# The mixer's last dense layer (1024 x 1024 x 1024, fp32 in three passes) as four pairs of output tiles of seven half-size products

## What is computed

```python
def _hybrid_mixer(h, w_in, ..., w_diff_out, w_fox_out, w_o, lambda_init):
    ...
    merged = jax.nn.sigmoid(ga) * (ya @ w_diff_out) + jax.nn.sigmoid(gb) * (yb @ w_fox_out)
    return merged @ w_o

def second_block(x, mem, ...):
        x = x + _hybrid_mixer(_rmsnorm(x, g_mix[l]), ...)
        x = x + _memory_cross_attention(_rmsnorm(x, g_mem_q[l]), _rmsnorm(mem, g_mem_kv[l]), ...)
        x = x + _sq_relu_mlp(_rmsnorm(x, g_mlp[l]), w1[l], w2[l])
```

## Time and profile before

| | us |
|---|---|
| median of 3 runs | 2438.28 |
| lowest, highest | 2435.59, 2439.02 |
| span of the profiled execution | 2433.8 |
| TensorE busy in the span | 2394.8 |
| VectorE, ScalarE, GpSimd busy | 1459.3, 951.4, 982.1 |

### The profile page before, as it was taken

One profiled execution on the slowest core, in us unless ns is written; L12 is line 12 of the kernel. 1 busy time (PEld: TensorE's weight loads), 2 busy tenths in 40 slices (PEclk: granted clock), 3 DMA queues, 4 the chain that ended last, 5 costly groups with the idle time before them and its releaser, 6 DMA issues. The chain is left out here.

```text
span 2433.8 us, 33823 instructions
## 1 busy us (share of the span) xinstructions
PE 2394.8 (98%) x12088; PEld 1995.5 (82%) x12088; DVE 1459.3 (60%) x2340; ACT 951.4 (39%) x1759; POOL 982.1 (40%) x776
## 2 busy tenths in 40 slices
PE   9999999999999999999999999999999999999998
PEld 4888888887888888888888888887877888888886
DVE  5865656476464446446454653445576666798878
ACT  4443434344133444434434520234243333444443
POOL 1323132222482222222222232311357666699785
PEclk9999999999999999999999999999999999999999
DMA  8513131223453221222122244211314444644442
GB/s 308 175 35 124 36 106 60 87 72 114 148 191 96 83 60 59 70 84 74 52 74 78 83 139 172 96 52 44 95 48 152 160 160 147 233 161 159 147 148 86
DMA packets 87144, 271.92 MB, mean 112 GB/s; under 512 B 10056, under 2 KB 10184, under 8 KB 82000
## 3 DMA queue, kind: packets, MB, share of 16 engines
q1 hardware_dynamic: 64560, 184.37, 22.7%
q10 hardware_dynamic: 22432, 85.60, 10.9%
HBM read 198.08 MB, written 58.23 MB: 105 GB/s over the span
## 5 line engine op out<-in xcount | busy, mean ns | idle before, releaser
L743 POOL CAST w_hi<-raw 128x1024 fp32r<-128x1024 f32 x112 | 120.5, 1076 | 1079.2 <-issue 369.7
L2999 PE MATMUL ps<-act_hi,w_hi 128*128 128x512 f32 x1248 | 499.0, 400 | 1.9 <-DVE act_lo L2641 1.1
L3001 PE MATMUL ps<-act_hi,w_lo 128*128 128x512 f32 x1248 | 488.5, 391 | 0.0
L3000 PE MATMUL ps<-act_lo,w_hi 128*128 128x512 f32 x1248 | 486.7, 390 | 0.0
L745 POOL TENSOR_TENSOR w_lo<-raw,w_hi 128x1024 fp32r<-128x1024 f32 x112 | 278.0, 2482 | 9.0
L3001 PEld LDWEIGHTS ps<-act_hi,w_lo 128*128 128x128 f32 x1248 | 234.2, 188 | 52.0
L2999 PEld LDWEIGHTS ps<-act_hi,w_hi 128*128 128x128 f32 x1248 | 234.6, 188 | 45.1 <-DVE act_lo L2641 1.5
L3000 PEld LDWEIGHTS ps<-act_lo,w_hi 128*128 128x128 f32 x1248 | 234.9, 188 | 40.6
L3015 PE MATMUL ps<-act_hi,w_hi 128*128 128x512 f32 x384 | 150.2, 391 | 1.6 <-POOL w_lo L745 1.2
L3017 PE MATMUL ps<-act_lo,w_hi 128*128 128x512 f32 x384 | 149.6, 390 | 0.0
L3019 PE MATMUL ps<-act_hi,w_lo 128*128 128x512 f32 x384 | 118.3, 389 | 0.0
(11 more groups left out here) (548 smaller groups left out, 5843.0 us busy)
## 6 DMA issues: line engine op xcount, KB each, us to landing
raw<-in_w_stream_dram SPq DMA_DIRECT2D x192, 512.0 KB, 3.6
x_own_f<-a_dram SPq DMA_DIRECT2D x32, 512.0 KB, 5.7
a_dram<-stage SPq DMA_DIRECT2D x18, 512.0 KB, 6.2
ada<-in_w_ada_dram SPq DMA_DIRECT2D x4, 2048.0 KB, 21.5
spill<-res ACTq DMA_DIRECT2D x16, 512.0 KB, 4.9
gate_dram<-gate_sb ACTq DMA_DIRECT2D x32, 256.0 KB, 2.0
stage<-spill ACTq DMA_DIRECT2D x16, 512.0 KB, 4.1
act_lo_f<-a_dram SPq DMA_DIRECT2D x16, 512.0 KB, 5.4
```

The lines of the kernel that those rows point to most:

```text
L743: nc.gpsimd.tensor_copy(w_hi[:, s, :, :], raw[:, s, :, :]).then_inc(S["w_hi"], 1)
L2999: nc.tensor.matmul(out, wh, xh, start=start, stop=False, skip_group_check=onto)
L3000: nc.tensor.matmul(out, wh, xl, start=False, stop=False, skip_group_check=onto)
L3001: return nc.tensor.matmul(out, wl, xh, start=False, stop=stop, skip_group_check=onto)
```

## The change

The layer `out = W^T X` is cut into 2 x 2 blocks: pairs of output tiles, halves of the channels (k 0 to 3, 4 to 7), halves of the tokens. Each pair takes seven products of 4 k, 128 outputs and 512 tokens in place of eight: with a11, a12 the halves of the first tile's weights and a21, a22 those of the second, s1 = a21 + a22, s2 = s1 - a11, s4 = s2 - a12, s3 = a21 - a11 on the weights, and on the operand t1 = x11' - x12', t2, t3, t5 from the halves of rows j and j+4. The products are numbered; `LP_ORDER = (1, 0, 4, 6, 3, 2, 5)` is the order on TensorE, `PLACE` gives each its bank, and 4, 6 and 5 add onto the banks of 1, 0 and 3.

- **Operand sums** (VectorE, `merged_row`): rows 0 to 3 write one sum each (L2817), rows 4 to 7 three each; of rows 0 to 3 only the left half gets a high and a low part. ScalarE makes highs of the sixteen sums (`t_hi`), GpSimd twelve of the lows (`t_lo`), VectorE four (`t_lows`). The sums lie in `res`, twelve of the highs and lows in memory that the merge's operand occupies until T_MERGE is done.
- **Weight sums** (GpSimd, `block_weights`): four sums and seven lows of 512 columns a pair; ScalarE makes the seven highs (`block_high`), before GpSimd did a cast and a subtraction of 1024 columns a tile. Most lie in the free right halves of `act_hi` and `act_lo` rows 0 to 3. `w_split` rises by two after the last low.
- **Read-out** (VectorE, `block_sums`): six reads of PSUM and three additions a pair; ScalarE copies product 1 out of its bank (`first_copied`) before product 4 adds onto it. x1 rows go to `x1_rows` and `stage` in turn (`x1_load`).
- **ScalarE's order**: the loops of the merge are unrolled and weight highs stand between the sigmoids; in block n it does `first_copied(n)`, squares and spills of block n-1, then all highs of block n+1. The mkv loads move behind the layer. New semaphores share counters of earlier stages (`lw_sum` is printed as qk_ss, `lw_hi` qk_sq, `lt_sum` qk_spread, `lt_hi` qk_perm, `lt_lo` qk_sin, `lp_done` qk_roped, `lp_copied` qk_normed, `lp_ev` df_pt).

```diff
-            split_range(T_MERGE + 2, 8)
-            split_range(T_WO + 2, 8)
+            for t in range(2, 8):
+                split((T_MERGE + t) // 2, t % 2)
+                if 3 <= t < 7:
+                    t_lo(0, t - 3)
+            def block_weights(n):
+                a11, a12, a21, a22 = (quarter(raw, o, h) for o in range(2) for h in range(2))
+                s1, s2, late, s3 = (lw_whole(n, i) for i in (0, 2, 6, 3))
...
+                loaded(0)
+                low(1, a11)
+                if n == 0:
+                    low(4, a12)
+                loaded(1)
+                summed(0, s1, a21, a22, ALU.add)
+                sum_made(0)
+                summed(2, s2, s1, a11, ALU.subtract)
+                if n:
+                    low(0, s1)
+                    low(4, a12)
+                sum_made(2)
+                summed(6, late, s2, a12, ALU.subtract)
...
+                low(3, s3)
+                low(2, s2)
+                if n == 0:
+                    for i, j in T_LOWS[4:]:
+                        t_lo(i, j)
+                pool.sem_inc(S["w_hi"], 2)
+                pool.wait_ge(S["lw_hi"], lw_high_count(n, 5))
+                nc.gpsimd.tensor_tensor(LP_LO[5], a22, LP_HI[5].bitcast(F), ALU.subtract).then_inc(S["w_split"], 2)
...
+                if i == 2:
+                    block_high(0, 1)
+                    block_high(0, 4)
+                    block_high(0, 0)
                 sigmoids(0, 2 * i + 2)
             sigmoids(1, 6)
+            block_high(0, 2)
+            block_high(0, 6)
+            block_high(0, 3)
             merged_hi(0, 6)
+            act.wait_ge(S["spilled"], 128)
+            act.wait_ge(S["tile_done"], T_WO)
+            x1_load(0)
...
+            for i, j in T_HIGHS[4:10]:
+                t_hi(i, j)
+            first_copied(0)
             merged_hi(1, 6)
+            for i, j in T_HIGHS[10:]:
+                t_hi(i, j)
+            block_high(0, 5)
...
+            for n in range(4):
+                if n:
+                    first_copied(n)
+                    for s in range(2):
+                        residual_square("wo", "x2", s, n - 1)
+                        residual_kept("wo", s, n - 1)
+                if n < 3:
+                    for i in (1, 0, 4):
+                        block_high(n + 1, i)
+                    if n:
+                        x1_load(n + 1)
+                    for i in (6, 3, 2, 5):
+                        block_high(n + 1, i)
...
+                read(0, 1, add[:, 1, right], add[:, 1, right], lp_bank(n, 0), ALU.subtract)
+                read(4, 2, res[:, a, left], add[:, 0, left], lp_bank(n, 4), ALU.add)
+                read(6, 3, res[:, a, right], add[:, 0, right], lp_bank(n, 6), ALU.subtract)
+                read(3, 4, add[:, 1, right], add[:, 1, right], lp_bank(n, 3), ALU.add)
+                read(2, 5, part, part, lp_bank(n, 2), ALU.add)
+                nc.vector.tensor_tensor(res[:, a, right], res[:, a, right], part, ALU.add).then_inc(S["lin_evac"], 1)
+                nc.vector.tensor_tensor(add[:, 1, left], add[:, 1, left], part, ALU.add).then_inc(S["lp_part"], 1)
+                nc.vector.tensor_tensor(res[:, b, right], add[:, 1, right], part, ALU.add).then_inc(S["lp_part"], 1)
+                nc.vector.tensor_tensor(res[:, b, left], add[:, 1, left], lp_bank(n, 5), ALU.add
+                                        ).then_inc(S["lin_evac"], 1)
...
-            with pe.Fori(0, 3) as i:
-                linear_pair("wo", T_WO, "merged", i)
-            linear_pair("wo", T_WO, "merged", 3, last=True)
+            def block_product(n, i):
+                out, onto = lp_bank(n, i), i >= 4
...
+                if i == 4:
+                    pe.wait_ge(S["lp_copied"], LEFT["lp_copied"] + n + 1)
+                elif i == 6:
+                    pe.wait_ge(S["lp_ev"], LEFT["lp_ev"] + 5 * n + 1)
+                elif i == 5:
+                    pe.wait_ge(S["lp_ev"], LEFT["lp_ev"] + 5 * n + 4)
+                for k in range(4):
+                    if n == 0 and i in (1, 4):
+                        pe.wait_ge(S["lo_ready"], 8 * FILL["merged"] + k + (1 if i == 1 else 5))
```

## The result

| | before | changed |
|---|---|---|
| median | 2438.26 us | 2453.02 us |
| lowest, highest (4 runs each) | 2435.59, 2439.02 | 2451.61, 2454.36 |
| span of the profiled execution | 2433.8 us | 2451.5 us |
| from the layer's first matmul to the query steps | 111.36 us | 126.46 us |

The ratio is 1.0062, with an interval from 1.0050 to 1.0074: slower, by 14.8 us. The prediction said 2452.1 with a range of 2437.0 to 2459.0.

What follows compares the result with a forecast made beforehand. TensorE, busy for 98% of the 2433.8 us span, was taken as the bound. Terms -10.9 + 7.8 + 6.5 + 3.5 + 5.2 + 1.7 = +13.8 gave a span of 2447.6 and, with 4.5 added, 2452.1 us; range 2437 to 2459.

Steps and rivals of the forecast that it cites:

- Block 0: First block of the layer: TensorE gets 7.8 us of new waiting at products 4 and 6.
- 0.8, 4.6 and 2.4: Block 0's waits in us: product 4 for ScalarE's copy, its k=3 for row 7's low half, product 6 for product 0's read.
- Block 1: Second block: product 4 waits 6.5 us for ScalarE's copy of product 1, which stands behind seven weight highs.
- Blocks 2 and 3: Weights run in a loop of 20.85 us against TensorE's 19.05; each block loses 1.8, together 3.5 us.
- 13.75 + 1.6 + 0.9: Within the weights' loop, in us: eleven GpSimd operations, two hand-overs to ScalarE and back, and meetings with VectorE.
- Into the next layer: From the last block to the query steps: late read, split, row 4 and last square add 5.2 us.
- the 6.0 counted: Waits into the query, in us, before taking off the 0.85 of old waiting that goes, leaving +5.2.
- The clock: Behind the last wait, one fall of the granted clock to half is not absorbed and costs 1.7 us.
- The conversion to a time: Forecast span 2447.6 us plus the kept 4.5 us between span and median of runs gives 2452.1.
- No blocking: Rival: VectorE and GpSimd do not hold each other up; time 2437.4 us, no measurable change; chance 0.15.
- Copy not late: Rival: block 1's weights land by 1480, no product 4 waits, gain nearly whole; 2427 to 2432 us; chance 0.05.
- Longer loop: Rival: GpSimd operations of the weights' loop cost 1.4 us, clock falls are not absorbed; 2457 to 2460 us; chance 0.22.

Runs made afterwards that it cites:

- e4: Changed kernel plus matmuls nobody reads where TensorE waits: 18 in block 0 ahead of row 7's low half, 16 in block 1 ahead of the copy; 2452.5 us, ratio 1.0058.
- e2: Changed kernel with row 6's sigmoid moved ahead of row 5's high, and so ahead of the three weight highs; 2452.0 us, ratio 1.0056.
- e6: Changed kernel with row 6's sigmoid ahead of row 5's high and row 6's high ahead of the weight highs for products 2, 6 and 3; 2454.5 us, ratio 1.0065.
- e1: Changed kernel with GpSimd giving the first raw tile of a block free once s3 is made, not with the last low; 2448.7 us, ratio 1.0051.
- e3: Changed kernel with ScalarE, in blocks 1 to 3, copying product 1 ahead of the highs for products 6, 3, 2 and 5; 2455.7 us, ratio 1.0072.
- e5: Changed kernel plus matmuls nobody reads: 6 ahead of the query's first tile, 5 ahead of the sums of squares; 2453.1 us, ratio 1.0064.
- e7: Changed kernel without GpSimd's eight lows of operand sums 3 and 2; ScalarE writes a copy of each sum instead; 2451.9 us, ratio 1.0058.
- e12: Against an earlier follow-up with reordered lists, VectorE in block 3 makes fewer lows ahead of its read of product 3 and all squares last; 2443.7 us, ratio 1.0028.

## Why the prediction was right

**The sum.** Positions from the layer's start, forecast and measured:

| | forecast | measured |
|---|---|---|
| VectorE starts row 6 | -6.1 | -6.16 |
| row 7's low half ends | 12.1 | 12.5 |
| product 4 of block 1 | 38.7 | 39.19 |
| product 4 of block 2 | 59.6 | 61.08 |
| product 4 of block 3 | 80.4 | 82.18 |
| sums of squares | 108.2 | 109.32 |
| query steps | 125.2 | 126.46 |

Rows 6 and 7, in VectorE's and ScalarE's timeline:

```profile
1460.64 2.36 DVE L2810 TENSOR_TENSOR gate_g<-ps,gate_g 128x1024 f32<-128x1024 f32 x2 [7.48 <-ACT gate_g L1695]
...
1468.37 1.78 DVE L2817 TENSOR_TENSOR res<-res 128x512 f32<-128x512 f32 x1
...
1476.98 2.28 DVE L2824 TENSOR_TENSOR act_lo<-stage,act_hi 128x1024 fp32r<-128x1024 f32 x1
...
1458.71 1.90 ACT L1695 ACTIVATE gate_g<-gate_g 128x2048 f32<-128x2048 f32 x1
```

These answer to the earlier trace rows, where the sigmoid stood at 1452.13 and VectorE began row 6 at 1454.90; this execution is 1.22 us later as a whole. A half-size sum takes 1.78 beside GpSimd, the full-size low half 2.28.

**Block 0: 7.8 forecast.** 0.8, 4.6 and 2.4 were measured as 0.51, 4.74 and 1.30. The third is smaller because the half clock had slowed TensorE before it; at full clock it is 2.57 (e4). Row 7's low half was late as forecast, but not by the sigmoid alone, which the forecast named: with the sigmoid moved (e2) the wait stays 4.75, and only with row 6's high moved too (e6) is it 1.68. And e6 shows what the sum didn't say: this block's waits are not a price of their own. Take them away and block 1 waits longer (6.34), because GpSimd's list gives the raw tiles free at nearly the same time.

**Block 1: 6.5 forecast, 4.29 measured,** with the product starting within 0.5 us of the forecast place. TensorE itself came 2.5 us later to it (block 1 began at 29.3, not 26.8), from the clock. The waits of both blocks are 10.84 us where the forecast has 14.3; the half clock and the restarts fill the rest. So the two terms were too large as waits, and right together as a position, because the weights and not TensorE set it.

**Blocks 2 and 3: a loop of 20.85 forecast, 21.89 and 21.10 measured.** GpSimd's last low of block 1, its first and last low of block 2; ScalarE's copies in blocks 1 and 2 and between them its first high of block 2:

```profile
1506.96 1.27 POOL L964 TENSOR_TENSOR w_lo<-raw,w_hi 128x512 fp32r<-128x512 f32 x1
1512.95 1.33 POOL L930 TENSOR_TENSOR act_lo<-raw,act_hi 128x512 fp32r<-128x512 f32 x1 [4.72 <-ACT act_hi L1735]
...
1528.88 1.29 POOL L964 TENSOR_TENSOR w_lo<-raw,w_hi 128x512 fp32r<-128x512 f32 x1
...
1505.36 0.58 ACT L1751 ACTIVATE first_part<-ps 128x512 f32<-128x512 f32 x1
...
1512.17 0.64 ACT L1735 ACTIVATE act_hi<-raw 128x512 fp32r<-128x512 f32 x1 [4.34 <-DMA raw<-in_w_stream_dram]
...
1527.25 0.58 ACT L1751 ACTIVATE first_part<-ps 128x512 f32<-128x512 f32 x1
```

From the end of the last low (1508.23) to the next first high 3.94 us, 0.78 to the first low, 17.22 to the end of the last: 21.94. The term that was too small is the list on GpSimd: 13.75 + 1.6 + 0.9 = 16.25 against 17.22. That the loop exists at all, the point of the term, is what e1 and e3 show.

**Into the next layer: 5.2 forecast.** The waits are 1.83 and 1.33, about half of the 6.0 counted, but a slow clock lies between them that the forecast did not have, and VectorE's last square sets the end (e5). From product 4 of block 3 to the steps the forecast has 44.8, the trace 44.3. I had put a wait at row 4, and there was none. The sum of this term is right, its parts are not.

**The clock: +1.7 for one fall that is not absorbed.** There were four falls worth some 8.9 us. e4 shows the first absorbed and e5 the third; for the second, in block 1, the evidence is only that the position of the next product is set by the weights. What is left is the fall behind the squares: from the first of them to the query steps it takes 17.14 us, and 15.45 in the kernel before, so 1.7. The step holds.

**The conversion to a time** was the weak one. The stage grew by 15.1, not 13.8. The span grew by 17.7: 1.2 more before the layer, nearly all of it before the merge, and 1.4 more behind the query steps, where TensorE's work is the same. And the profiled execution of before was its fastest run (2435.59; its span is 1.8 less, and 1.8 is the distance in all four runs of the changed kernel too), so the "4.5" between span and median was 1.8 of overhead and 2.7 of difference between runs. The span came out 3.9 us higher than forecast (2451.5 against 2447.6), the distance to the median 3.0 us smaller (1.5 against 4.5), and so the time was off by 0.9 only. That the two errors cancel is luck; by its stage alone the forecast was 1.3 us short.

**What was to be seen in the profile.** 336 matmuls, the sigmoid of row 6 behind a weight high, waits of 4 to 7 us in blocks 0 and 1 and under 3 after, half-size operations near 1.7, a clock below 1.00: all there. The layer is 97.94 us, not about 95: 1.8 us of the difference stand ahead of product 4 of block 3, and the layer so measured ends with the query's wait, which the 95 did not hold.

**The rivals.** No blocking: falls with e7. Copy not late: 4.29 us of waiting. Longer loop: its turns are longer by 1.0 and 0.3 us, where the rival had 3 x 1.6, and the clock's falls are absorbed; a quarter of it came true.

## What to carry to other kernels

When a product is saved on the engine that bounds, add up what VectorE and GpSimd get for it, and price their operations as they run beside each other. Here 10.9 us of TensorE cost 31 us more of VectorE and 40 of GpSimd in the layer, and a wait that an edit took away was in most cases met again at a later product, until the last one stood behind the layer. Free a load buffer at its last reader, not at the end of the list: that gave 6.5 us of the stage. And read a stage by its positions from its own start, not by the waits: waits move, positions add up.

## What the runs showed of the hardware

- VectorE with two SBUF inputs and 512 columns: 0.69 us with GpSimd idle, mostly 1.64 to 1.78 beside it (e7 and the changed kernel); 1024 columns 1.23 and 2.28 to 2.34. Beside a GpSimd low of 1024 columns it loses more: 2.83 us for one of 512 columns in the changed kernel (at 95.59 from the layer's start), 3.18 for a square of 1024 in e12. GpSimd's half-size operation goes from 1.25 to 1.77 where VectorE's list is full (e6, eight in 14.19 us), so it loses about half of what VectorE does, as the forecast had it.
- A fall of the granted clock to 0.50 came in or behind waits of 4.7, 4.3, 1.8 and 1.3 us in the changed kernel, but not at its wait of 1.76 at 1548.98, nor at one of 1.33 in e1 (1502.70) or one of 2.57 in e4 (1483.37). The length of the wait alone doesn't tell, and what does stays open here. (The Trainium skill, page TensorE: Matmul & The Clock Gate, section Why this matters for your kernels, warns of long idle gaps between bursts, which bring the half rate back. The trace agrees at the waits of 4.74 and 4.29; the falls behind 1.83 and 1.33 came after shorter waits than it warns of.)
- A fall is not of one length for one kernel either: in block 0 the clock is down from 1476.6 to 1486.9 in the changed kernel, and only from 1477.2 to 1480.6 in e5, which is the same up to there and waits as long.
- A fall costs nothing that the noise of 0.7 us lets one see where the next wait is set by another engine (e4 in block 0, e5 at the query's first tile).
